# A hybrid decoder block on one core: w_out streamed twice beside the retrieval, once for the second token tile and once for the last two

## The chip, the cores and the metric

The kernel is one program on one core of a Trainium2 chip, everything in fp32. The time is the device time of one execution in microseconds (us). The engines are TensorE (PE, with its weight loads PEld), VectorE (DVE), ScalarE (ACT), GpSimd (POOL) and the sync engine SP, which issues transfers; all transfers run on the core's 16 DMA engines.

## What is computed

There are 512 tokens of width 2048 (four tiles of 128 tokens). The part of the reference that matters here, after attention and the convolution branch:

```
merged = sigmoid(gates)[attn] * attn + sigmoid(gates)[conv] * conv     # gates: h @ w_in (4096 columns)
y = merged @ w_out                                                     # 2048 x 2048
x = x + gate1 * rms_norm(y, g[1])
h = rms_norm(x, g[2]) * (1 + scale2) + shift2
q = h @ w_q                                                            # 2048 x 2048
s1, s2 = q halves . sub_keys; top-16 of each, top-16 of the 256 sums   # per token and head: 16 experts, 8 heads
act = gelu(h . expert_down[idx]) * softmax(top)
out = x + gate2 * rms_norm(act @ expert_up[idx], g[3])
```

For each token 128 rows of 2048 numbers are gathered from expert_down and 128 from expert_up, both tables in HBM.

## The kernel before

**Retrieval.** The 512 tokens are 512 blocks: one block gathers 128 rows of 8 KB from the down table (a [128, 2048] tile) and 128 from the up table. Positions within a block hold pairs of tokens and experts so that 32 blocks (a group J) finish 32 tokens. GpSimd issues the gathers in one order (down of block i, then up of block i - 22, L595). VectorE does one dot per block (`dot`, L1636), ScalarE the GELU and the small diagonal weights (L1173), TensorE the weighted sum of up rows (`weighted_rows`, 24 positions behind the dot). At each 32nd position `h2_quarter` turns 32 tokens of h into rows in four steps that alternate between TensorE and ScalarE (L1161), and the next dot waits for them. The gathers go into rings of three slots each, and of five from block WIDE = 168 on, which also waits for the end of the tail.

**Tails.** What lies between attention and the queries runs per token range, weights streamed from HBM in chunks of 1 MB through a ring of three (`rows`, `put` on SP; `group` on PE). `tail(0)` handles tile 0 (128 tokens), before any retrieval. `tail(1)` handles tiles 1 to 3 (384 tokens) while tile 0's 128 blocks are retrieved: for four column groups cg the gates ga and gc (w_in), the branch projections ao and co; then four groups of the output projection "out" (w_out, 16 chunks); then the norm chain: root of the sum of squares, scaling of y (L1732), residual with the turned x rows ("x", L1739), squares of the new x (L1260), their sums (PE), scaling (L1748), modulation (L1265). Then the queries "q" and scores "sc" (w_q, 16 chunks) for tile 1, each group of which VectorE routes at once (`route`, six steps, and `gates`); and again "q2" and "sc2" for tiles 2 and 3, which are routed later, each beside the blocks of the tile before it: from block 36 of the tile on, one pair of heads per 23 blocks (ROUTE, STRIDE), a step every second block.

**Order.** All engines run in program order. `block_pace` makes a table PACE: after chunk i of tail(1) every engine advances the retrieval up to position PACE[i] (`chunk_out` on PE, `passed` on ACT and DVE), by a weight per chunk: 12 for ga, gc, co and out, 6 for ao, 9 for x, 4 for q. Blocks 0 to 128 are spread over all chunks up to the first four of q, 763 units; 12 more chunks of q take blocks 128 to 138, the 16 chunks of q2 blocks 138 to 162. SP only stores finished rows between chunks (`behind`).

## Time and profile before

| | |
|---|---|
| median of 3 runs (us) | 4072.42 (4071.71 to 4079.16) |
| profiled execution (us) | 4070.52 |
| its span (us) | 4068.7 |
| busy: PE, PEld, DVE, ACT, POOL (us) | 2782.0, 1644.1, 2275.8, 539.8, 1408.8 |
| moved by DMA | 1430.07 MB, mean 351 GB/s |
| mean granted TensorE clock | 0.772 of 2.4 GHz |

A time "into the span" counts from the first instruction. Block 0's dot starts at 1159.86 us, block 128's at 2018.74, the first of the last tile (384) at 3371.88, and the last one at about 4001. In views of stretches "(x)" is a count of instructions; a product in fp32 is two instructions on PE. The share of DMA can be slightly above 1.

### The profile page before, as it was taken

Reading aid. Unit: us, or ns where it says so; the run is one execution under the profiler, and the core shown is the slowest. Engines: PE = TensorE matmul, PEld = TensorE weight load, DVE = VectorE, ACT = ScalarE, POOL = GpSimd, SP = SyncE. Lnnn points to the kernel's source line nnn. Section 1 sums busy time; section 2 is a strip of 40 time slices with the busy share of each in tenths; the row PEclk is TensorE's granted clock in tenths of the full one; section 3 lists DMA queues with packets and bytes.
Section 4 is the critical chain, followed back from the end, with each engine's and each line's share of the span. In section 5 each row is a group of like instructions: output and inputs, shape, how many; then the busy total and the mean of one; then the engine's idle time right before and its main releaser. Section 6 shows DMA issues by size and latency. Waiting matters only on the chain.

```text
span 4068.7 us, 38721 instructions
## 1 busy us (share of the span) xinstructions
PE 2782.0 (68%) x15652; PEld 1644.1 (40%) x15652; DVE 2275.8 (56%) x3525; ACT 539.8 (13%) x1203; POOL 1408.8 (35%) x1109
## 2 busy tenths in 40 slices
PE   5899899889899999998779344443443444444435
PEld 3687788789855554554657010110110100101100
DVE  5399789743474443435673666654656664444442
ACT  3211221200210011111211010010010100100000
POOL 2421211010023444333133563444435434444342
PEclk8999999999999999999989555555555555555556
DMA  9353424698669999999799999999999999999998
GB/s 365 144 218 134 156 90 170 239 407 342 223 243 373 400 419 397 414 379 400 282 370 402 400 422 421 421 421 422 421 421 419 415 422 416 421 422 419 422 421 368
DMA packets 204145, 1430.07 MB, mean 351 GB/s; under 512 B 24640, under 2 KB 24768, under 8 KB 32192
## 3 DMA queue, kind: packets, MB, share of 16 engines
q0 software_dynamic: 152064, 1107.36, 65.8%
q1 hardware_dynamic: 45984, 308.30, 19.5%
q10 hardware_dynamic: 5920, 11.94, 0.8%
q8 instruction: 124, 2.03, 0.2%
q14 instruction: 53, 0.43, 0.0%
HBM read 1420.13 MB, written 7.39 MB: 351 GB/s over the span
## 4 chain that ended last, share of the span: by engine, by line
PE 41%; DMA 39%; DVE 12%; POOL 3%; issue 3%; ACT 2%; ACTq 0%; DVEq 0%; SPq 0%; POOLq 0%
PE psum L624 40%; DMA front<-in_down,back 27%; DMA front<-in_up,back 10%; DVE front L1636 3%; POOL front L595 3%; DVE back L1403 2%; DVE back L1372 1%; DMA front<-in_w_in 1%; DMA back<-in_ada_w 1%; ACT back L1161 1%; DMA back<-in_up,back 1%; DMA back<-in_x 1%; DMA front<-in_w_conv_o 0%; DVE back L1739 0%; ACT front L1265 0%
## 5 line engine op out<-in xcount | busy, mean ns | idle before, releaser
L624 PE MATMUL psum<-front 128*32 128x512 f32 (+3 forms) x7136 | 1384.9, 615 | 862.9 <-DMA front<-in_up,back 793.9
L1636 DVE CUSTOM_DVE_ANT_0 front<-front,back 128x2048 f32<-128x2048 f32 x512 | 1171.1, 2292 | 1308.8 <-DMA front<-in_down,back 1201.6
L624 PEld LDWEIGHTS psum<-front 128*32 128x32 f32 (+1 forms) x7136 | 627.0, 162 | 1558.3 <-issue 1336.3
L595 POOL DMA_INDIRECT front<-in_down,back x512 | 606.7, 1185 | 897.7 <-DVE back L1636 626.2
L595 POOL DMA_INDIRECT front<-in_up,back x444 | 531.7, 1197 | 900.8 <-PE psum L624 860.5
L624 PE MATMUL psum<-back,front 128*32 128x128 f32 (+3 forms) x4384 | 625.5, 445 | 296.9 <-DMA back<-in_up,back 169.0
L624 PEld LDWEIGHTS psum<-back,front 128*32 128x32 f32 (+1 forms) x4384 | 365.0, 163 | 565.9 <-issue 317.2
L573 POOL TENSOR_TENSOR w_low<-front,w_high 128x2048 fp32r<-128x2048 f32 x33 | 153.7, 4657 | 539.7 <-ACT w_high L1049 539.7
L624 PE MATMUL psum<-x_high,w_high 128*128 128x512 f32 x640 | 252.0, 394 | 8.4 <-POOL x_low L579 5.6
L624 PE MATMUL psum<-x_low,w_high 128*128 128x512 f32 x640 | 250.6, 392 | 0.0
L624 PE MATMUL psum<-x_high,w_low 128*128 128x512 f32 x640 | 250.5, 391 | 0.0
L624 PE MATMUL psum<-back 128*32 128x128 f32 (+5 forms) x1400 | 181.7, 390 | 57.6 <-ACT back L1260 14.8
L1173 ACT ACTIVATE front<-back 128x32 f32<-128x32 f32 x512 | 116.1, 308 | 725.8 <-DVE back L1645 725.8
L624 PEld LDWEIGHTS psum<-back 128*128 128x128 f32 (+1 forms) x1400 | 134.9, 184 | 135.6 <-issue 56.6
L1372 DVE SCALAR_TENSOR_TENSOR back<-back 128x512 f32<-128x512 f32 x232 | 160.3, 766 | 0.0
L1049 ACT ACTIVATE w_high<-front 128x2048 fp32r<-128x2048 f32 x52 | 99.6, 1916 | 454.7 <-PE psum L624 405.5
L1403 DVE SCALAR_TENSOR_TENSOR back<-back 128x512 f32<-128x512 f32 x120 | 145.1, 1209 | 7.0 <-DMA back<-in_ada_w 1.5
L624 PEld LDWEIGHTS psum<-x_high,w_high 128*128 128x128 f32 x640 | 121.3, 189 | 34.8 <-POOL x_low L579 6.2
L624 PEld LDWEIGHTS psum<-x_high,w_low 128*128 128x128 f32 x640 | 121.1, 189 | 25.6
L624 PEld LDWEIGHTS psum<-x_low,w_high 128*128 128x128 f32 x640 | 121.2, 189 | 24.8
L1161 ACT ACTIVATE back<-psum 128x512 f32<-128x512 f32 x64 | 38.2, 597 | 515.0 <-DVE back L1636 359.7
L595 POOL DMA_INDIRECT back<-in_up,back x68 | 74.1, 1090 | 91.9 <-PE psum L624 87.3
(160 smaller groups left out, 1672.5 us busy)
## 6 DMA issues: line engine op xcount, KB each, us to landing
front<-in_w_in SPq DMA_DIRECT2D x116, 1024.0 KB, 8.4
back<-in_ada_w SPq DMA_DIRECT2D x64, 1024.0 KB, 7.8
front<-in_w_q SPq DMA_DIRECT2D x48, 1024.0 KB, 6.9
front<-in_ada_rows POOLq DMA_DIRECT2D x32, 1024.0 KB, 13.1
front<-in_w_out SPq DMA_DIRECT2D x32, 1024.0 KB, 8.0
front<-in_w_conv_o SPq DMA_DIRECT2D x16, 1024.0 KB, 9.4
front<-in_w_attn_o SPq DMA_DIRECT2D x16, 512.0 KB, 8.8
front<-in_down,back POOLq DMA_INDIRECT x512, 20.8
```

What stands on the lines that cost most here:

```text
L573: nc.gpsimd.tensor_tensor(wl[s], ring[s], wh[s % 2].bitcast(fp32), ALU.subtract).then_inc(w_low_done, 1)
L595: nc.gpsimd.indirect_dma_start(out=row_, out_offset=None, in_=table[:, :], in_offset=bass.IndirectOffsetOnAxis(ap=idx4[:, t % 2, c:c + 1], ...
L624: return nc.tensor.matmul(o, a, b, start=start, stop=stop)
L1049: A(wh[s % 2], ring[s], ACT.Copy).then_inc(w_high_done, 1)
L1161: A(h2r[:, i * NT:(i + 1) * NT], ps[:, 7, :], ACT.Copy).then_inc(h2r_ready, 1)
L1173: A(diag[:, b % 32, :], same[:, 0:32], ACT.Copy, scale=actv[:, n % 2, b % 16:b % 16 + 1]).then_inc(diag_ready, 1)
L1372: last[c] = st.did(V.scalar_tensor_tensor(total, src, tap, total, ALU.mult, ALU.add))
L1403: ins = V.scalar_tensor_tensor(total, part, weight, total, ALU.mult, ALU.add)
L1636: V.tensor_tensor_reduce(d_row[s], d_row[s], h2r, 1.0, 0.0, ALU.mult, ALU.add, pre[:, b // 16 % 2, b % 16:b % 16 + 1]).then_inc(dots_done, 1)
```

## The change

The out groups, the x rows and the norm chain move into the loop over query ranges (QUERIES): for tile 1 alone first, then for tiles 2 and 3 together as "out2", x, q2, sc2. w_out is streamed once for each range, so three times in the kernel instead of twice. tail(1) has 115 chunks instead of 99. The pace changes with it: 617 units carry blocks 0 to 128, an out chunk of tile 1 has weight 4; the chunks of q for tile 1 carry the same blocks as before; out2's 16 chunks blocks 138 to 162, the two x chunks up to 164 and 167, q2's 16 chunks up to 191. The rings widen at block 200, routing of tiles 2 and 3 starts at block 64 of the tile before, one pair of heads per 15 blocks. The cut diff (ScalarE's and VectorE's parts are moved into the same loop in the same way, with `goes` counting ranges for the semaphore values):

```diff
-    out += [("out", i, 4) for i in range(4)] + [("x", t, 1) for t in range(TAIL[c][1] // P)]
-    for go, _, _ in QUERIES[c]:
+    for go, q0, qn in QUERIES[c]:
+        out += [("out" + go, i, 4) for i in range(4)]
+        out += [("x", t, 1) for t in range(q0 // P, (q0 + qn) // P)]
         out += [(kind + go, i, k) for i in range(4) for kind, k in (("q", 4), ("sc", 0))]
...
-WIDE = 168
+WIDE = 200
-ROUTE, STRIDE = 36, 23
+ROUTE, STRIDE = 64, 15
...
-    work = [k * (12 if kind in ("ga", "gc", "co", "out") else 6 if kind == "ao" else 9 if kind == "x" else 4) / max(k, 1)
-            for kind, _, k in tail_groups(1) for _ in range(k)][:-28]
+    work = [k * (12 if kind in ("ga", "gc", "co") else 6 if kind == "ao" else 9 if kind == "x" else 4) / max(k, 1)
+            for kind, _, k in tail_groups(1) for _ in range(k)][:-46]
     out = [round(128 * at / sum(work)) for at in itertools.accumulate(work)]
     out += 4 * [128] + [129, 130, 131, 132, 133, 135, 136, 138]
-    return out + [138 + 3 * (i + 1) // 2 for i in range(16)]
+    out += [138 + 3 * (i + 1) // 2 for i in range(16)] + [164, 167]
+    return out + [167 + 3 * (i + 1) // 2 for i in range(16)]
...
# SP
-                for i in range(4):
-                    for s in range(4):
-                        rows(w_out, i, s)
+                for _, q0, qn in QUERIES[c]:
+                    for i in range(4):
+                        for s in range(4):
+                            rows(w_out, i, s)
+                            behind(c)
+                    for t in range(q0 // P, (q0 + qn) // P):
+                        put(x_row, x[t * P:(t + 1) * P, :])
                         behind(c)
...
# PE
-                    if i == 0:
-                        pe.wait_ge(mix_ready, 16 * (c + 1))
-                        group(4, 4, mixT, mix_at, dve_took, VTOOK[c, "co", 3], before)
-                    else:
-                        group(4, 4, mixT, mix_at, act_took, ATOOK[c, "out", i - 1], before)
+                        if i:
+                            group(4, 4, mixT, mix_at, act_took, ATOOK[c, "out" + go, i - 1], before, tq)
+                        elif go:
+                            group(4, 4, mixT, mix_at, act_took, ATOOK[c, "sc", 3], before, tq)
+                        else:
+                            pe.wait_ge(mix_ready, 16 * (c + 1))
+                            group(4, 4, mixT, mix_at, dve_took, VTOOK[c, "co", 3], before, tq)
...
# DVE, retrieve
-                        if step == 20:
+                        if step == 14:
                             gates(t, n)
...
# DVE, tail: only the first range of a tail is routed in it
+                    for i in range(4):
                         passed(c, 4)
+                        if not go:
+                            dve.wait_ge(act_took, ATOOK[c, "sc", i] + 4)
+                            for step in range(6):
+                                route(c, i, step)
```

## Rows read from the trace of the kernel before

**Rows 1.** The page: GB/s moved in each of 40 equal slices.
```profile
GB/s 365 144 218 134 156 90 170 239 407 342 223 243 373 400 419 397 414 379 400 282 370 402 400 422 421 421 421 422 421 421 419 415 422 416 421 422 419 422 421 368
```

**Rows 2.** Stretches: length, busy us of each engine (instructions), clock, DMA share, GB/s.
```profile
1150.00:1170.00 20.00, 20.00 (x64) 11.79 (x63) 15.99 (x45) 1.17 (x1) 5.59 (x3) 1.00 0.35 122
1170.00:1260.00 90.00, 90.00 (x281) 52.95 (x280) 54.57 (x71) 8.00 (x21) 28.64 (x20) 1.00 0.88 337
...
1320.00:1340.00 20.00, 17.85 (x190) 10.06 (x192) 7.54 (x7) 5.17 (x7) 6.50 (x4) 1.00 0.79 315
1340.00:1500.00 160.00, 159.28 (x652) 82.19 (x645) 65.19 (x69) 17.90 (x51) 67.89 (x54) 1.00 1.01 419
1500.00:1550.00 50.00, 47.85 (x298) 25.73 (x298) 21.69 (x26) 3.89 (x6) 14.84 (x12) 1.00 0.92 375
...
1700.00:1800.00 100.00, 97.32 (x515) 52.24 (x514) 33.86 (x32) 14.25 (x38) 37.01 (x28) 1.00 0.95 375
...
1940.00:1970.00 30.00, 15.23 (x93) 11.40 (x92) 13.74 (x9) 12.80 (x23) 1.88 (x2) 0.77 0.15 57
1970.00:2100.00 130.00, 108.08 (x849) 85.85 (x846) 103.58 (x385) 18.89 (x60) 35.14 (x27) 0.89 0.94 377
...
2120.00:2230.00 110.00, 104.13 (x576) 78.71 (x575) 40.70 (x38) 14.11 (x49) 40.82 (x34) 1.00 1.01 422
2230.00:2260.00 30.00, 14.00 (x189) 5.85 (x187) 9.23 (x9) 5.68 (x15) 12.55 (x11) 0.76 0.70 283
2260.00:4000.00 1740.00, 718.66 (x4430) 161.89 (x4430) 970.35 (x1485) 158.68 (x486) 784.33 (x694) 0.54 1.01 420
...
1150.00:1900.00 750.00, 735.60 (x3156) 392.52 (x3154) 314.17 (x357) 81.82 (x210) 291.89 (x220) 1.00 0.95 387
```

**Rows 3.** Timeline: start, us, engine, line; a block, a 384-column chunk, a 256-column chunk's loads.
```profile
1503.45 1.07 PE L624 MATMUL psum<-front 128*32 128x512 f32 x8
1504.45 10.59 PE L624 MATMUL psum<-back,front 128*128 128x384 f32 x32
...
2222.41 6.77 PEld L624 LDWEIGHTS psum<-front 128*128 128x128 f32 x32 [0.84 <-issue]
```

**Rows 4.** Groups by shape, 1958 to 1978: four chunks of 128 columns.
```profile
L624 PE MATMUL psum<-front 128*128 128x128 f32 x128 | 16.7, 295 | 14.8 <-ACT front L1265 14.8
```

**Rows 5.** Transfers issued, 1150 to 1900.
```profile
front<-in_w_out SPq DMA_DIRECT2D x16, 1024.0 KB, 8.5
```

**Rows 6.** Timeline of the norm chain of 384 tokens.
```profile
1905.19 6.76 DVE L1732 TENSOR_TENSOR front<-front,back 128x1536 f32<-128x1536 f32 x4
1911.99 4.22 DVE L1739 SCALAR_TENSOR_TENSOR back<-front,back,psum 128x128 f32<-128x128 f32 x16
...
1932.05 12.06 PE L624 MATMUL psum<-back 128*128 128x384 f32 x32 [7.78 <-ACT back L1260]
...
1949.14 9.68 ACT L1265 ACTIVATE front<-front,back 128x384 f32<-128x384 f32 x16 [4.41 <-DVE front L1748]
...
1965.65 0.94 POOL L595 DMA_INDIRECT front<-in_up,back  x1 [35.38 <-PE psum L624]
```

**Rows 7.** Timeline of VectorE: the dots of blocks 20, 127, 128, 160 and 192.
```profile
1252.79 2.28 DVE L1636 CUSTOM_DVE_ANT_0 front<-front,back 128x2048 f32<-128x2048 f32 x1
...
1977.64 2.29 DVE L1636 CUSTOM_DVE_ANT_0 front<-front,back 128x2048 f32<-128x2048 f32 x1 [19.11 <-DMA front<-in_down,back]
...
2018.74 2.29 DVE L1636 CUSTOM_DVE_ANT_0 front<-front,back 128x2048 f32<-128x2048 f32 x1
...
2238.47 2.29 DVE L1636 CUSTOM_DVE_ANT_0 front<-front,back 128x2048 f32<-128x2048 f32 x1 [10.28 <-ACT back L1161]
...
2405.88 2.29 DVE L1636 CUSTOM_DVE_ANT_0 front<-front,back 128x2048 f32<-128x2048 f32 x1 [6.29 <-ACT back L1161]
```

**Rows 8.** Stretches of 10 us, columns as in rows 2.
```profile
2110.00:2120.00 10.00, 5.45 (x18) 3.20 (x19) 4.60 (x4) 0.00 (x0) 8.55 (x5) 0.53 1.00 413
2170.00:2180.00 10.00, 8.00 (x44) 6.18 (x40) 3.67 (x4) 1.11 (x4) 4.66 (x4) 1.00 1.01 422
```

More of the change, by code:

```diff
@@ L941, in squares @@
                     for i in range(count):
-                        ins = mm(ps[:, 6, 0:n], ones, buf[:, i, 0:n], first and i == 0, last and i == count - 1)
+                        ins = mm(ps[:, 6, 0:buf.shape[2]], ones, buf[:, i, :], first and i == 0, last and i == count - 1)
                     return ins
@@ L968, in tail @@
                         modulation_columns(2)
-                for i in range(4):
-                    def before():
-                        if i:
-                            pe.wait_ge(act_took, ATOOK[c, "out", i])
-                            squares(sqt, 4, i == 1, False).then_inc(sqs_used, 1)
-                    if i == 0:
-                        pe.wait_ge(mix_ready, 16 * (c + 1))
-                        group(4, 4, mixT, mix_at, dve_took, VTOOK[c, "co", 3], before)
-                    else:
-                        group(4, 4, mixT, mix_at, act_took, ATOOK[c, "out", i - 1], before)
-                    if c == 0 and i == 0:
-                        modulation_columns(3)
@@ L982, in tail @@
-                pe.wait_ge(act_took, ATOOK[c, "out", 3] + 4)
-                squares(sqt, 4, False, True).then_inc(ss_done, 1)
-                for t in range(t0 // P, (t0 + n) // P):
-                    r = x_row[chunk_in()]
-                    for m in range(4):
-                        if t > t0 // P:
-                            pe.wait_ge(dve_took, VTOOK[c, "x", t - t0 // P - 1] + m + 1)
-                        for k in range(4):
-                            ins = nc.tensor.transpose(ps[:, m, k * P:(k + 1) * P], r[:, (4 * m + k) * P:(4 * m + k + 1) * P], ident)
-                        ins.then_inc(g_done, 1)
-                    chunk_out(c)
@@ L1204, in retrieve @@
                         z_std(J)
[L1205 removed]
+                    t, at = b // 128 + 1, b % 128 - ROUTE - 10
                     if 2 <= t < TT and at >= 0 and at % STRIDE == 0 and at < 4 * STRIDE:
@@ L1241, in tail @@
                     passed(c, 5)
-                for i in range(4):
-                    passed(c, 3)
-                    for m in range(4):
-                        act.wait_ge(g_done, DONE[c, "out", i] + m + 1)
-                        A(hT[:, 4 * i + m, tok], ps[:, m, 0:n], ACT.Copy)
-                        if i == 0 and m == 0:
-                            act.wait_ge(mix_ready, 16 * (c + 1))
-                        if i and m == 0:
-                            act.wait_ge(sqs_used, 10 * c + i)
-                        A(sqt[:, m, 0:n], ps[:, m, 0:n], ACT.Square).then_inc(act_took, 1)
-                    passed(c, 1)
@@ L1744, in tail @@
-                dve.wait_ge(std2_ready, 2 * c + 2)
-                dve.wait_ge(dve_took, VTOOK[c, "x", n // P - 1] + 4)
-                st.link(V.reciprocal(row[:, 0:n], row[:, 0:n]))
-                for i in range(4):
-                    V.tensor_tensor(hT[:, 4 * i:4 * i + 4, tok], mixT[:, 4 * i:4 * i + 4, tok],
-                                    row[:, 0:n].unsqueeze(1).to_broadcast(wide), ALU.mult).then_inc(h2n_ready, 1)
-                for i in range(4):
-                    passed(c, 4)
-                    dve.wait_ge(act_took, ATOOK[c, "sc", i] + 4)
-                    for step in range(6):
-                        route(c, i, step)
-                    if i:
-                        gates(c, i - 1)
```

137 lines of the change are left out of this document (86 added, 51 removed).

## The prediction

> **What bounds the kernel now.** I read the page's slices first [rows 1]: from slice 24 of 40 on the rate stays at about 421 GB/s. From 2260 us to 4000 us the transfers are the bound: 420 GB/s over 1740 us [rows 2]. A block there costs 2.10 MB (128 rows of 8 KB from each table), which is 4.97 us at 422 GB/s. What can move is therefore how many bytes the kernel carries, and how long the queues stand below 422 GB/s before 2260 us.
>
> The stage table [rows 2] gives that second sum. The lost time of a stretch is its length times (1 - rate/422). 1150 to 1170: 14.2 us; 1170 to 1260: 18.1; 1320 to 1340: 5.1; 1500 to 1550: 5.6; 1700 to 1800: 11.1; the rest up to 1900 about 8, so that the one row of 1150 to 1900 (387 GB/s) gives 62. Then 1940 to 1970: 26.0 (57 GB/s); 1970 to 2100: 13.9; 2120 to 2230: nothing; 2230 to 2260: 9.9. That is some 112 us up to 2260. Outside that total nothing is to be had from moving work.
>
> TensorE looks as bound as the queues in the second tail: 735.6 us busy of 750 [rows 2]. Its piece costs [rows 3]: a chunk of 16 products of 384 tokens 10.59 us as one piece (10.24 us from start to start at 0.32 us per instruction), a block 1.07 us. A chunk with its 2.01 blocks is then 12.4 us of TensorE, and 1.05 + 2.01 x 2.10 = 5.27 MB or 12.5 us of DMA. The two limits coincide: taking TensorE work out of this stretch lets it run no faster than 422 GB/s.
>
> **The change, part by part.**
>
> *The extra load.* w_out is streamed twice beside the retrieval instead of once: 16 more chunks of 1024 KB (the stretch before shows 16 of them, the page 32 in all) [rows 5], 16.8 MB, at 422 GB/s **+39.8 us**. All of it goes into a stretch that ran at 422 GB/s (2120 to 2230) or into new stretches of the same kind, so no idle bandwidth hides it. The x rows are loaded as often as before, only later; the third load of w_q was there already (48 chunks). Bounds 35 to 40: the lower one if a chunk or two fall into the gaps that remain.
>
> *Gates, branches and the first tile's output projection (up to the first norm chain).* By the pacing formula the 128 blocks are now spread over 617 units instead of 763, so a 12-unit chunk has 2.49 blocks, not 2.01. Per chunk DMA is 1.05 + 2.49 x 2.10 = 6.27 MB, 14.9 us; TensorE 10.24 + 2.66 = 12.9 us. The out chunks have 128 columns (16.7 us for four, so 4.2 us each [rows 4]) and 0.83 block: 5.1 us of TensorE against 6.6 us of DMA. TensorE gets slack of about 2 us a chunk, but the bytes up to the chain are the same. What is recovered is only lost DMA time. In 1170 to 1260 VectorE halts after block 19 until the first branch sum is ready; block 20 starts at 1252.79 [rows 7], behind ten chunks of TensorE work, and the rate falls there. It will have up to five more dots to do before that wait, 5 more gathers of 1.05 MB, 12 us at most; I take 9. The stalls at each 32nd block (1320, 1500, 1700 stretches, 21.8 us together) come from four copies in series, some 7 us, behind a full chunk; with bursts of 2.5 blocks more is in flight when they begin, with rings of the same three slots. I take 8 of the 21.8. The 14.2 us before the first gathers stay. Sum **-17 us**; bounds 0 (three-slot rings refill no better, or bursts of three blocks drain them) and -45 (everything but the 14.2 and 3 of the rest goes).
>
> *The first chain (norm of y, residual, norm of x2, modulation), now for 128 tokens.* Before [rows 6]: scaling 6.76 from 1905.19 on, three residual groups of 4.22 with dots between, eight squares with their sums 12.06, then reciprocal and second scaling, modulation 9.68 us up to 1958.8: with the root and the reciprocal ahead of the scaling some 60 us. GpSimd waited 35.38 us for TensorE before its next up gather, because the gathers are issued in order; queued work lasted about 10 us of it, and 26.0 us were lost. With a third of the tokens: 0.9 + 2.4 + one group 4.2 + sums about 6 + 0.9 + 0.6 + modulation 4.5, plus semaphores about 3: 23 us, and a gap between up gathers of about 20 us. Less the 10 us (up to 17 with the rings freshly requested) 3 to 10 us stay lost: **-20 us**; bounds -15 and -26.
>
> *Routing of the second tile* (from block 127 at 1977.64 to block 138, about 2100) has the same instructions in the same order in both. Two routes and a gates step fill VectorE from there to block 128 at 2018.74 [rows 7]. Its loss, 13.9 us, stays: **0** (+-3).
>
> *The second projection, for 256 tokens, beside blocks 138 to 162.* Per chunk TensorE has 6.8 us (weight loads of one chunk in the last query group [rows 3]) plus 1.5 blocks, 8.4 us; DMA 1.05 + 1.5 x 2.10 = 4.2 MB, 9.95 us. Exactly this mix ran at 422 GB/s and clock 1.00 [rows 2]. TensorE's, ScalarE's and VectorE's work of this part costs nothing while that holds; the cover gone, it would be 16 x (8.4 - 5.1), 53 us of TensorE, less what the first part gave up.
>
> *The second chain, for 256 tokens, between blocks 162 and 168.* It is new as a stall. 1 + 1.7 + 4.5 + 4.2, then two dots, 4.2, three dots (2.29 each, but 5 us each by DMA); squares 8 x 1.03; 0.8 + 1.7 + 1.1; modulation 16 x 0.42 = 6.7 us; then one chunk of 6.8 us before the next block. Between up gathers lies a gap of 21 to 29 us. With the same 10 to 17 us of queued transfers: **+12 us**; bounds +4 (dots and gathers interleave so well that all is covered) and +26 (what the chain lost before).
>
> *Block 192's stall.* The turning of rows at each 32nd block meets three-slot rings at 160 and 192 now, since the rings grow to five slots at block 200, not 168. At 160, where the weights ended, it cost 9.9 us (the dot idle 10.28 us behind ScalarE [rows 7]). Now the end of the weights falls on 192 and costs that, and 160 has weights in flight: **+4 us**; bounds 0 and +9.
>
> *Routing of tiles three and four, 15 blocks a head pair instead of 23.* Steps stay two blocks apart within a pair. Two routes and a gates step took 39 us [rows 7], so about 18 us each, 21 with gates: 4 x 21 + 60 dots x 2.29 = 221 us in 60 blocks x 4.97 = 298 us. Rings of five slots and DMA hide it: **0**; bounds 0 and +4.
>
> Sum: 39.8 - 17 - 20 + 12 + 4 = **+19 us**. The profiled execution took 4070.5 us (span 4068.7), the median of the runs is 4072.4, 1.9 above it. So 4089.5 in the profile, **4091 us** as a median.
>
> A page differs from a row here. The rate of mixed weights and gathers is 422 GB/s [rows 2]. The Trainium skill, "DMA: Bandwidth & Descriptors", Where 436 GB/s comes from, says that transfers between HBM and SBUF are held by the HBM side at about 358 GB/s per core. By that the reload would be an estimated 46.9 us and the sum +26; the trace's 422 decides.
>
> **Rivals.** (a) *The first stretch was starved by TensorE* and the queues fill once it has slack. For it: 735.6 of 750 us busy, and losses scattered in it. Then -45 there, -26 for the first chain and +4 for the second: 39.8 - 45 - 26 + 4 + 4 = -23 us, 4049 us. It decides as soon as the first part recovers over 36 us at my other terms. Against: the stretch 1340 to 1500, 160 us long, loses 1 us as it is. (b) *The second chain costs what the first did.* Nothing of it is covered, because GpSimd's in-order gathers stop with TensorE: 39.8 - 10 - 15 + 26 + 9 = +50 us, 4122 us. For it: the 35.38 us wait. Against: 256 tokens and blocks inside it. (c) *TensorE's clock falls in the new 128-column out chunks*, where it now waits for weights. With TensorE busy 5.45 of 10 us the granted clock was 0.53 of 2.4 GHz, near the 1.2 GHz level; with 8.00 of 10 us it was 1.00 [rows 8]. The share would be 5.1 of 6.6, between them, nearer the second. At 1.2 GHz a chunk has 8.4 + 0.83 x 2.14 = 10.2 us against 6.6: 16 x 3.6 = +57 us, 4148 us at worst, half of it if the clock comes and goes. The Trainium skill, "TensorE: Matmul & The Clock Gate", HAM oscillation, says that when the products of a slice are shorter than the wait for the next slice, each slice starts at the low clock; by that rule this rival holds. Against it stands the second projection's mix at clock 1.00, whose TensorE share is 8.4 of 9.95. (d) *The change doesn't do what it says:* the gates stretch follows TensorE's removed work (16 x 6.1 = 98 us shorter). The coincidence of both limits excludes nearly all of this.
>
> **Numbers.** About 0.2% (8 us) can be told from no change. My forecast's own terms, 4075 to 4105: 0.60; (a), or a part of it that ends below 4064: 0.15; between them, near no change: 0.10; (b): 0.10; (c) 0.04; (d) 0.01. The range, 4056 to 4120, takes in the nearer half of (a) and of (b). Of the forecast's share about 0.1 lies within 0.2%: faster 0.16, same 0.20, slower 0.64.
>
> **What would show it.** The free run from block 200 on must keep 4.97 us a block and 420 GB/s. The bytes rise by 16.8 MB, from 1430 to 1447. The stretch before the first chain ends 5 to 20 us sooner (last square at 1880 to 1895 instead of about 1898) with DMA at 395 GB/s or more. The wait of GpSimd in the first chain falls from 35 to about 20 us. A second gap of GpSimd of 20 to 30 us appears between blocks 162 and 168, near 2230 us. Block 192 comes at about 2425 us, against 2405.88 [rows 7], and the difference stays the same to the end. I am wrong if the first stretch shortens by more than 35 us, if the second chain shows no dip, if the clock falls below 0.8 in the out stage, or if the later blocks run slower than 5.02 us.

## The result and the profile after

The changed kernel took 4120.58 us (median of 4 runs, 4113.18 to 4121.15) beside 4074.18 of the kernel before: ratio 1.011 [1.0097, 1.0122], some 46 us slower. The forecast was +19 us and 4091; the direction was right, the size was not. The profiled execution, 4113.18 us with a span of 4111.4, was the shortest of the four, so the profiles differ by 42.7 us in span. A further set of runs of the same kernel gave 1.0089 [1.0075, 1.0102] (e5 below).

The page of the changed kernel: GB/s in 40 slices, the transfers as a whole, and one issue row.
```profile
GB/s 366 139 225 130 154 102 146 270 404 330 206 273 396 416 376 414 374 421 361 381 392 395 353 381 419 419 421 422 421 421 420 418 421 417 419 421 420 421 422 368
DMA packets 206455, 1446.94 MB, mean 352 GB/s; under 512 B 24896, under 2 KB 25024, under 8 KB 32448
...
front<-in_w_out SPq DMA_DIRECT2D x48, 1024.0 KB, 8.7
```
w_out is issued 48 times and the bytes rose by 16.87 MB, as forecast. Beside [rows 1] the slices agree within 3 GB/s from slice 25 on, so the difference lies before about 2500 us.

Stretches of the changed kernel, with the columns of [rows 2].
```profile
1150.00:1170.00 20.00, 20.00 (x63) 11.78 (x62) 18.94 (x57) 1.95 (x3) 4.10 (x2) 1.00 0.19 63
1170.00:1260.00 90.00, 80.86 (x247) 46.42 (x246) 55.81 (x68) 8.93 (x26) 38.04 (x27) 0.94 0.98 387
...
1500.00:1550.00 50.00, 45.52 (x260) 24.61 (x261) 16.48 (x16) 5.71 (x9) 20.05 (x16) 0.93 0.87 349
1690.00:1800.00 110.00, 91.02 (x465) 48.87 (x462) 42.31 (x45) 10.64 (x27) 41.79 (x34) 0.91 0.93 379
1150.00:1900.00 750.00, 658.12 (x3169) 369.56 (x3168) 319.04 (x372) 79.57 (x216) 280.78 (x223) 0.94 0.96 390
1900.00:1940.00 40.00, 17.75 (x124) 14.26 (x122) 25.99 (x41) 11.85 (x34) 4.86 (x6) 0.66 0.70 292
1940.00:1970.00 30.00, 29.85 (x259) 26.78 (x258) 16.29 (x60) 2.80 (x11) 2.82 (x3) 1.00 0.90 343
1970.00:2100.00 130.00, 98.82 (x708) 73.16 (x707) 102.01 (x344) 19.87 (x60) 48.08 (x35) 0.84 0.94 377
2100.00:2210.00 110.00, 102.82 (x606) 75.77 (x608) 38.41 (x36) 14.81 (x46) 38.87 (x32) 0.98 1.01 421
2210.00:2240.00 30.00, 19.97 (x152) 10.02 (x143) 23.37 (x44) 3.17 (x5) 12.88 (x11) 0.73 0.87 352
2240.00:2260.00 20.00, 9.98 (x40) 6.18 (x40) 12.76 (x14) 9.04 (x15) 3.75 (x4) 0.76 1.00 415
2260.00:2280.00 20.00, 14.33 (x57) 11.16 (x58) 5.44 (x5) 7.32 (x20) 1.88 (x2) 0.73 0.18 64
2300.00:2420.00 120.00, 116.11 (x641) 86.20 (x643) 45.31 (x42) 20.59 (x75) 42.10 (x36) 0.97 1.01 421
2420.00:2480.00 60.00, 23.49 (x216) 7.74 (x208) 33.27 (x75) 9.66 (x27) 25.53 (x21) 0.59 0.88 353
2480.00:4040.00 1560.00, 641.23 (x3980) 144.99 (x3980) 875.30 (x1353) 142.29 (x427) 717.18 (x625) 0.54 1.01 420
```
The free run kept its 420 GB/s. Read as lost time (length times (1 - rate/422)): the stretch up to 1900 lost 57 us against 62; the first chain (1900 to 1970) 17.9 against 29 by the same reading of the kernel before; routing (1970 to 2100) 13.9 against 13.9; the second output projection nothing; the stall at block 160 (2210 to 2240) 5.0 against 9.9; the new second chain (2260 to 2280) 17.0; block 192 (2420 to 2480) 9.8, where the kernel before lost nothing (421 and 422 GB/s from 2380 to 2440). The table in the prediction leaves out two stretches of the kernel before: 1900 to 1940 (390 GB/s, 3.0 us) and 2100 to 2120 (306 GB/s, 5.5 us); with them its 112 us agree with the 120.3 below.

Two rows cover the whole stretch, the first of the kernel before, the second of the changed one.
```profile
1150.00:2560.00 1410.00, 1131.24 (x5736) 619.35 (x5738) 724.65 (x1267) 171.28 (x466) 560.39 (x430) 0.87 0.95 386
```
```profile
1150.00:2560.00 1410.00, 1142.19 (x6178) 699.67 (x6176) 682.94 (x1159) 186.08 (x521) 522.63 (x412) 0.88 0.94 385
```
Lost time 120.3 and 123.6 us. The balance closes: 16.87 MB at 422 GB/s, 40.0 us, and 3.3 us more of lost time make 43.3; block 256 came 44.0 us later, block 511 42.7. The forecast had 21 us less lost time, net, and it became 3 us more. Note what such a balance is: bookkeeping. Every run moved 420 GB/s from 2560 to 4000, so the bytes and the lost time before 2560 have to add up to the delay. It says where the time went; it doesn't say why.

The norm chains of the changed kernel in the timeline: first the one of 128 tokens, then the one of 256.
```profile
1909.43 2.29 DVE L1642 CUSTOM_DVE_ANT_0 front<-front,back 128x2048 f32<-128x2048 f32 x1 [7.02 <-DMA front<-in_down,back]
...
1912.63 2.50 DVE L1740 TENSOR_TENSOR front<-front,back 128x512 f32<-128x512 f32 x4
...
1915.16 4.22 DVE L1747 SCALAR_TENSOR_TENSOR back<-front,back,psum 128x128 f32<-128x128 f32 x16
...
1927.90 6.26 ACT L1274 ACTIVATE front<-front,back 128x128 f32<-128x128 f32 x16 [1.75 <-DVE front L1756]
...
1934.21 12.05 PE L626 MATMUL psum<-front 128*128 128x128 f32 x79 [8.46 <-ACT front L1274]
...
1942.02 0.94 POOL L597 DMA_INDIRECT front<-in_up,back  x1 [19.21 <-PE psum L626]
...
2221.29 4.63 DVE L1740 TENSOR_TENSOR front<-front,back 128x1024 f32<-128x1024 f32 x4
...
2245.84 8.12 PE L626 MATMUL psum<-back 128*128 128x256 f32 x32
...
2257.64 7.98 ACT L1274 ACTIVATE front<-front,back 128x256 f32<-128x256 f32 x16 [3.08 <-DVE front L1756]
...
2265.67 24.66 PE L626 MATMUL psum<-front 128*128 128x256 f32 x110 [11.71 <-ACT front L1274]
...
2276.73 0.94 POOL L597 DMA_INDIRECT front<-in_up,back  x1 [26.86 <-PE psum L626]
...
2285.71 2.29 DVE L1642 CUSTOM_DVE_ANT_0 front<-front,back 128x2048 f32<-128x2048 f32 x1 [20.27 <-DMA front<-in_down,back]
```
GpSimd's wait in the first chain fell from 35.38 [rows 6] to 19.21 us, as forecast, and a second one of 26.86 appeared. The dots [rows 7] have as counterparts in the changed kernel:
```profile
1953.20 2.29 DVE L1642 CUSTOM_DVE_ANT_0 front<-front,back 128x2048 f32<-128x2048 f32 x1 [19.11 <-DMA front<-in_down,back]
...
1994.31 2.29 DVE L1642 CUSTOM_DVE_ANT_0 front<-front,back 128x2048 f32<-128x2048 f32 x1
...
2214.89 2.29 DVE L1642 CUSTOM_DVE_ANT_0 front<-front,back 128x2048 f32<-128x2048 f32 x1 [8.68 <-ACT back L1165]
...
2440.40 2.29 DVE L1642 CUSTOM_DVE_ANT_0 front<-front,back 128x2048 f32<-128x2048 f32 x1 [8.68 <-ACT back L1165]
```
Blocks 127 and 128 came 24.4 us sooner, 160 23.6 sooner, 192 34.5 later, and 200 42.0 later (2440.8 and 2482.7).

Two cautions on reading such positions. First, a block is a measure of progress only where both kernels have moved the same other bytes ahead of it. At block 128 nearly all is equal (16 w_out chunks issued since 1150 in both), but of x the kernel before has loaded three rows of 1 MB and the changed one only one: the other two now come behind block 162. These 2.1 MB are 5.0 us that moved and weren't won. So about 19 us of lost time were won up to there, which agrees with the rates (869 us at 375 GB/s lost 96.8, 844 us at 383 GB/s 78.0). Second, single profiles scatter. Nine profiles whose code is the changed kernel's up to block 128 have it 19.2 to 27.7 us sooner than the profile of the kernel before (mean 23.3), and five of the kernel before, with the same code up to there, have it 0 to 9.3 us later (mean 6.1). By the means the lead is 29 us and not 24.

### The profile page after: what moved, and what is told of

It reads as the page before. It is cut to its first block, busy times and chain, and to the rows that moved or that the text cites. A ratio compares the mean times of both kernels' runs of the same rounds, so it can differ in the third digit from the quotient of the medians.

```text
span 4111.4 us, 39974 instructions
## 1 busy us (share of the span) xinstructions
PE 2807.4 (68%) x16228; PEld 1732.3 (42%) x16228; DVE 2277.0 (55%) x3535; ACT 558.8 (14%) x1268; POOL 1406.7 (34%) x1109
## 4 chain that ended last, share of the span: by engine, by line
DMA 42%; PE 35%; DVE 12%; POOL 5%; issue 3%; ACT 2%; ACTq 0%; DVEq 0%; POOLq 0%
PE psum L626 35%; DMA front<-in_down,back 29%; DMA front<-in_up,back 10%; POOL front L597 4%; DVE front L1642 3%; DMA back<-in_up,back 2%; DVE back L1378 1%; DVE back L1409 1%; DMA front<-in_w_in 1%; ACT back L1165 1%; POOL x_low L581 1%; DVE back L1620 1%; DMA back<-in_x 1%; ACT front L1274 0%; DVE back L1578 0%
## 5 line engine op out<-in xcount | busy, mean ns | idle before, releaser
L626 PEld LDWEIGHTS psum<-front 128*128 128x128 f32 (+1 forms) x7184 | 632.0, 161 | 1549.0 <-issue 1302.2
L626 PE MATMUL psum<-back,front 128*32 128x128 f32 (+4 forms) x4848 | 645.3, 424 | 311.7 <-DMA back<-in_up,back 154.0
L626 PEld LDWEIGHTS psum<-back,front 128*32 128x32 f32 (+1 forms) x4848 | 439.4, 173 | 543.5 <-issue 334.5
L626 PE MATMUL psum<-back 128*32 128x128 f32 (+5 forms) x1464 | 184.0, 381 | 53.5 <-ACT back L1269 12.3
```

Of the source, the lines that this page charges most:

```text
L626: return nc.tensor.matmul(o, a, b, start=start, stop=stop)
```

## Experiments

Ratios are to the kernel before, run on the same chip. "Balance" is (bytes over those of the kernel before)/422 plus the change of lost time between 1150 and 2560 (each good to about 2 us, since rates have whole GB/s), beside how much later block 256 was in the profile. The runs that are not in the table have their times in the text.

| run | median us | ratio [95%] | lost us | balance | block 256 |
|---|---|---|---|---|---|
| before | 4074.18 | 1 | 120.3 | 0 | 0 |
| changed | 4120.58 | 1.011 [1.0097, 1.0122] | 123.6 | +43 | +44.0 |
| e5 again | 4116.21 | 1.0089 [1.0075, 1.0102] | 123.6 | +43 | +44.3 |
| e1 small reload | 4108.16 | 1.0077 [1.0059, 1.0095] | 153.7 | +36 | +37.6 |
| e9 light products | 4122.01 | 1.0101 [1.0084, 1.0118] | 133.6 | +53 | +53.5 |
| e10 both | 4103.41 | 1.0057 [1.004, 1.0073] | 150.4 | +33 | +35.4 |
| e3 retrieval in chains | 4108.38 | 1.0077 [1.0059, 1.0095] | 120.3 | +40 | +40.3 |
| e11 split chain | 4120.00 | 1.0098 [1.0081, 1.0114] | 170.4 | +50 | +48.3 |
| e12 split, covered | 4086.64 | 1.0019 [1.0009, 1.0029] | 137.0 | +17 | +16.6 |
| e13 widened at 193 | 4123.27 | 1.0113 [1.0098, 1.0129] | 133.6 | +53 | +53.5 |
| e14 covered, paced | 4114.64 | 1.0091 [1.0077, 1.0105] | 123.6 | +43 | +44.9 |
| e16 covered, 1.25 | 4121.35 | 1.0104 [1.0088, 1.0121] | 123.6 | +43 | +43.4 |
| e17 covered, 1.75 | 4099.57 | 1.0065 [1.0051, 1.0079] | 106.9 | +27 | +27.7 |
| e18 uncovered, 1.75 | 4119.49 | 1.0102 [1.0087, 1.0116] | 133.6 | +53 | +54.4 |

The balance closes in every row within 3 us, as it must while the free run keeps its rate. What remains to be found is what sets the lost time.

**The changed kernel again: e5,** on another chip, without an edit.


> The changed kernel once more, to have its time on the chip of the other three of this group. Theory: 4118 to 4122; if it comes out near 4110, part of what the first group of experiments seemed to win (12 us each) was only the chip.

Its span was 4110.6 us and its blocks stood where they stood in the first profile (block 192 34.4 us late, block 256 44.3), so the shift is the kernel's. The ratio puts it at 36 to 46 us.

**Is it the bytes or the work? e1, e9, e10.** e1 loads only a corner of each w_out chunk of out2; e9 has a quarter of its products; e10 does both.
```diff
-                            rows(w_out, i, s)
+                            if go:
+                                put([r[:, 0:1, 0:P] for r in tring], w_out[i, s][:, 0:1, 0:P])
+                            else:
+                                rows(w_out, i, s)
...
-  group(4, 4, mixT, mix_at, act_took, ATOOK[c, "sc", 3], before, tq)
+  group(4, 1, mixT, mix_at, act_took, ATOOK[c, "sc", 3], before, tq)
```


> The changed kernel, but the 16 chunks of w_out for the last two tiles are loaded as 64 KB instead of 1024 KB each (128 columns of one k; the products run as before on what else lies in the buffers, so the last two tiles' projection is wrong). 15.7 MB less. Theory A (the added bytes are paid in full, because the queues are the bound wherever no chain stops them): 37 us less than the changed kernel's 4120, so 4083, with about the same lost DMA time. Rival B (the added time is late routing, late widening of the rings and TensorE's rearranged work, the bytes fall into gaps): 4105 or more.

> The changed kernel with only one of the four products per chunk and output column block in the second projection (16 chunks of w_out for the last two tiles: 64 instead of 256 products, all bytes loaded; the projection of those tiles is then incomplete). Theory F (the second projection meets two limits at once, TensorE at 8.9 us and the queues at 9.95 us a chunk with its 1.5 blocks, so that taking one away wins next to nothing): 0 to 6 us less than the changed kernel. Rival G (TensorE alone is the bound there): 20 us or more less.

> The same with, in addition, the 16 chunks loaded as 64 KB each. Theory F: now both limits are gone, 24 blocks take some 120 us instead of 155, so 30 to 38 us less than the changed kernel, some 4080; the sum of the two single experiments (about 10 us) is far exceeded. Rival G: about as much as taking the products alone.

e1 took away 15.7 MB, 37 us of transfers, and won 5 to 13 us (1.0077 against the 1.0089 and 1.011 of the changed kernel). Its stretches:
```profile
2100.00:2140.00 40.00, 40.00 (x208) 29.39 (x207) 16.19 (x15) 3.59 (x12) 21.49 (x14) 1.00 0.96 364
2140.00:2200.00 60.00, 59.11 (x354) 44.40 (x356) 22.21 (x21) 9.97 (x32) 22.14 (x19) 1.00 0.95 368
```
Without the bytes TensorE is busy for 99.11 of 100 us and DMA drops to 364 and 368 GB/s. e9, without the work, kept 422 GB/s with TensorE busy 57.66 of 110 us and won nothing, as expected. In e10 both limits were lifted, and still only 13 to 21 us came, not the 30 to 38 expected: blocks 144 to 156 ran at about 5.1 us each, but the second chain behind them stalled as before (255 GB/s from 2240 to 2290). So the second output projection stands on both limits at once, and half of the price or more (23 of 36 to 46 us) is left without it.

**The two small edits: e2, e6, e7** (each to the kernel before).
```diff
-WIDE = 168                 # e2, e6
+WIDE = 200
-ROUTE, STRIDE = 36, 23     # e2, e7, with the steps that follow from it
+ROUTE, STRIDE = 64, 15
```


> The kernel before with only the constants of the change: rings widen at block 200 instead of 168, routing of tiles 3 and 4 from block 64 at one head pair per 15 blocks, its gates at step 14. Theory A: routing is hidden, the three-slot rings cost up to 9 us at block 192; 4074 to 4083. Rival B (late routing and late widening carry a good part of the 46 us): 4090 or more.

> The kernel before with the rings widened at block 200 instead of 168, nothing else. Theory C (the 9 us of the constants come from the turning of rows at block 192 meeting rings of three slots): 4081 to 4084. Rival D (they come from denser routing steps): 4074 to 4076.

> The kernel before with routing of tiles 3 and 4 from block 64 on at one head pair per 15 blocks, rings widened at 168 as before. Theory C: 4073 to 4077, since five slots and the queues hide routing. Rival D: 4081 to 4084.

e2 gave 4085.2 us, 1.0022 [1.0012, 1.0032]; e6 4090.31, 1.002 [1.0011, 1.0029]; e7 4081.43, 1.0001 [0.9992, 1.001]. Late routing is free, as forecast; late widening costs the kernel before 8 us. In e6's profile it appears at one place: the difference is 9.6 us at block 192, all of which was there at block 160 already, before the edit acts, and 15.7 at block 196. The up ring widens by its own block number, 22 places later in GpSimd's order than the down ring: WIDE = 168 put it at place 190, just ahead of the turning of rows at 192, WIDE = 200 puts both rings behind it. Which of the two rings matters wasn't separated.

**The first chain: e4 and e3.** Both retrieve blocks inside the chain, where the code otherwise lets TensorE and ScalarE wait; e4 is the kernel before with it, e3 the changed one, in both chains.
```diff
+                    if c == 1:
+                        retrieve(170 if go else 128)
```


> The kernel before with the same continuation up to position 128 in its one chain of 384 tokens. Theory A: of the 26 us lost at 1940 to 1970 about 14 are won, 4060. Rival B: no difference, 4072 to 4076.

> The changed kernel with the retrieval going on inside both norm chains of the second tail: after the eight sums of squares TensorE, and after the second root ScalarE, go on to position 128 (first chain) or 170 (second) before they wait for the modulated h. Theory A (the queues run empty in the chains because the next up gather waits for TensorE, which stands in its program order at the query product): GpSimd's waits of 19.2 and 26.9 us shrink to 5 to 12 us, 15 to 25 us are won, 4098. Rival B (VectorE's residual, dots and scaling hold the gathers as long as TensorE does): under 5 us won, 4116 or more.

e4: 4072.82 us, 0.9995 [0.9985, 1.0004], nothing. Block 127 came 14.3 us sooner (1963.3), block 128 1.8 us later: the likely reason is that from block 127 on the path is VectorE's routing, which begins when the chain's queries are there, so that gathers covered in the chain are waited for anyway. In e3 block 170 came 19.6 us sooner than in the changed kernel (15.3 ahead of the kernel before instead of 4.3 behind), and at block 192 only 4 us of that were left; of the 15 to 25 us expected at the end, 5 to 13 came by the ratios.

**A chain split without a second load: e8, e11, e12.** w_out is loaded once, for 384 tokens; only the norm chain and the queries are split in two ranges. e8 retrieves inside both chains and keeps 14 blocks back for them; e11 is the plain form; e12 adds retrieval inside both chains, a pace that follows it, and an up ring that widens at GpSimd's place 176.
```diff
-WIDE = 173
+WIDE, UWIDE = 176, 154
-    out += [123, 124, 126, 127, 128] + 4 * [128] + [129, 130, 131, 132, 133, 135, 136, 138]
-    return out + [140, 143] + [143 + 3 * (i + 1) // 2 for i in range(16)]
+    out += [123, 127, 127, 128, 128] + 4 * [128] + [129, 130, 131, 132, 133, 135, 136, 138]
+    return out + [141, 144] + [148 + 3 * (i + 1) // 2 for i in range(16)]
+MID = {"": (124, 126), "2": (146, 148)}      # retrieve(MID[go][..]) behind squares 4 and 8
```


> w_out streamed once for all 384 tokens as in the kernel before, but the norm chain and queries in two ranges as in the change (tile 1, later tiles 3 and 4 beside blocks 138 to 172), with the retrieval going on inside the chains and 114 instead of 121 blocks ahead of the first; rings widen at 180, routing from block 48, one head pair per 19 blocks. Theory A (the shorter first chain stands on the path to the second tile's routing and its 25 us are real; what the change loses is the second projection with its reload, 40 to 50 us of queue and TensorE time in one): block 128 some 30 us sooner than in the kernel before, 10 to 18 us kept at the end, 4056 to 4066. Rival E (the second chain and the pieces around it give back all that the first wins, whatever the reload): 4072 or more.

> The change without its second projection: w_out streamed once, for 384 tokens, paced as before; the norm chain and queries in two ranges as in the change (x and chain of tiles 3 and 4 between blocks 138 and 143, their queries up to 167), rings widened at 173, routing from block 44, one head pair per 20 blocks. Theory A: block 128 about 25 us sooner than in the kernel before, the second chain costs 15 to 18, late widening 5: within 5 us of the kernel before, and some 40 us under the changed kernel. Rival E (the split chain itself is what costs): 4090 or more.

> The same with the retrieval going on inside both chains (to 124 and 126, to 146 and 148, the pace of the last 16 chunks moved up by as much) and the ring of the up rows widened at its block 154, that is at position 176 together with the other one instead of 22 positions later. Theory A: the second chain's stall mostly gone and nothing lost at block 192: 10 to 18 us under the kernel before, 4058 to 4066. Rival: as e11.

e8: 4106.63 us, 1.0064 [1.0052, 1.0077], nothing of the hoped gain: blocks kept back did not speed a stretch in which TensorE was busy 723.41 of 750 us (1170 to 1920), and block 128 came 5.6 us later than in the kernel before, where 30 us sooner was expected. e11: 4120.00 us where a time near the kernel before was expected. It carries the bytes of the kernel before and costs what the change costs: its second chain stands behind routing in VectorE's order, DMA moved 259 GB/s from 2060 to 2140, and from block 138 to block 148 it fell back by 22.7 us (from +7.0 to +29.7 against the kernel before). e12 (the diff is against e11; its routing starts at 48, one pair per 19 blocks) took 33 us off that, with the same bytes and the same arithmetic: 11 us of it stood at block 138, behind the first chain, 41 at block 148. It is still 8 us slower than the kernel before, where 10 to 18 us faster was expected. So most of what e11 costs depends on how the stalls are covered, though cover, pace and ring widening changed together here.

**The second chain of the changed kernel itself: e13 to e18.** e13 only widens the rings as the tail ends; e15 widens the kernel before's up ring where its down ring widens.
```diff
-WIDE = 200
+WIDE, UWIDE = 193, 171      # e13; e15: 168, 146
```


> The changed kernel with the five-slot rings as soon as its second tail ends: the down ring at block 193 instead of 200, the up ring at the same place of GpSimd's order (index 171 instead of 200, which was place 222). In the changed kernel alone a comparison of the old tile with both settings gave +6 us at blocks 192 to 196. Theory W (the late widening costs 8 us in the changed kernel too): block 200 comes 5 to 9 us sooner than in the changed kernel and the gain stays; ratio to before 1.007 to 1.0085, that is 4109 to 4115 us beside a before of 4081. Theory V (the stall of block 192 falls on three-slot rings in either case, since the second tail ends at block 191, so that only what follows can gain): 0 to 3 us, ratio 1.009 to 1.011.

> The kernel before with the up ring widened where the down ring is (GpSimd's place 168, not 190). If the three-slot up ring behind block 168 costs anything in it, block 192's stall of 9.6 us shrinks by 2 to 6 us: ratio 0.9985 to 0.9995. If the widening only has to come ahead of the turn at block 192 (place 190 does), nothing: ratio 0.9995 to 1.0005.

e13 won nothing and its block 192 was worse (2420 to 2460 lost 13.7 us by its rows of 330 and 225 GB/s, the changed kernel 9.8). Its trace shows a likely reason: GpSimd stood idle for 14.83 us ahead of the gather at 2450.82, until VectorE's dot of block 192 (2448.26 to 2450.55). With WIDE = 193 the widened down ring begins with slot 0, which block 192 had taken just before, so block 193's rows couldn't be requested until that dot was done, and the other table's gathers stood behind it. With 200 slot 0 was last taken by block 198, one block further back. e15: 4077.94 us, 1.0003 [0.9994, 1.0012], no effect; the ring only has to be wide ahead of the turn. So this way of widening early doesn't win back the stall at 192; a setting without the clash of slots wasn't run.

e14, e16 and e17 put retrieval to blocks 169 and 171 inside the second chain (e14 in the first too). They differ in the pace of the 16 query chunks behind it: 1.5, 1.25 and 1.75 blocks each. The down ring widens at 196, 200 and 204, the up ring at the same place of GpSimd's order. e18 is 1.75 without the retrieval, widened at 200.
```diff
-    return out + [167 + 3 * (i + 1) // 2 for i in range(16)]
+    return out + [171 + 5 * (i + 1) // 4 for i in range(16)]   # e16; e14: 3 // 2; e17: 7 // 4; e18: 167 + 7 // 4
+MID = (169, 171)
+                        if go and kk % 4 == 3:
+                            retrieve(MID[kk // 4])
```


> The changed kernel with both w_out loads, but with retrieval steps inside its second chain (to block 169 behind the fourth square, to 171 behind the last), the pace of the last query chunks moved behind them (the second tail ends at block 195, not 191), and the up ring widened at GpSimd's place 196. In the split kernel with one load of w_out the same edits took away 33 us. Theory S (the new second chain with its drained three-slot rings is, beside the bytes, what the change costs): the same edits take 20 to 30 us here too; ratio 1.003 to 1.005, 4093 to 4101 us beside a before of 4081. Theory T (the second output projection with its bytes and products is what costs, and the queues are given no room to catch up): 0 to 10 us, ratio 1.008 to 1.010, as when only the retrieval was continued.

> The changed kernel with its first chain as it is and retrieval inside the second chain only (to block 169 behind the fourth square, to 171 behind the last); the 16 last query chunks have 1.25 blocks each behind block 171, so that the second tail ends at block 191 as in the changed kernel; down ring widened at 200 as there, up ring at the same place of GpSimd's order instead of 222. In e14 the window 2210 to 2300 lost 8 us of transfers against 23 in the changed kernel, but the first chain, where retrieval was also put, lost 9.5 more (block 128 at -14.9 against -24.4) and the 192 turn 5 more. Theory S (the second chain's stall is worth some 15 us once the queues have something behind it): block 200 at +24 to +30 against before, ratio 1.0055 to 1.0075, 4099 to 4107 us beside a before of 4076. Theory T (the chain's loss is a catch-up that TensorE, busy all the time afterwards, gives back): block 200 at +38 to +42, ratio 1.009 to 1.011.

> As e16, but 1.75 blocks instead of 1.25 for each of the 16 last query chunks behind block 171 (the second tail ends at block 199); routing of the later tiles from 72 on, 14 blocks a head pair; rings widened at 204. In e16 the chain was covered (block 172 at -19.4 against before, the changed kernel +10.6), and then TensorE was busy for 100.00 of 100 us from 2280 to 2380 at 313 to 421 GB/s and all was given back by block 192. Theory U (both limits coincide behind the chain, so the covered stall is worth something only if DMA and not TensorE is the limit afterwards): with 1.75 blocks a chunk DMA wants 11.2 us a chunk and TensorE about 9.9; the queues keep 420 GB/s to block 192, and block 208 comes at +22 to +32 against before, ratio 1.005 to 1.0075. Theory T (the stall is always given back, by another stall at the end of the tail): block 208 at +38 or more, ratio 1.009 or more.

> The changed kernel with its chain uncovered and only the pace of the last 16 query chunks at 1.75 blocks (end of the tail at block 195, routing from 68, 14 blocks a head pair, rings widened at 200). Behind the chain the changed kernel already ran at 422 GB/s for 120 us, so both theories expect next to nothing: block 208 at +36 to +44, ratio 1.009 to 1.0115. If it were much faster (under 1.007), TensorE would have been the limit behind the uncovered chain too.

The cover worked each time: block 170 came at -9.0, -18.6 and -19.7 us against the kernel before (e14, e16, e17), where the changed kernel has +4.3. What became of it was decided behind the chain. Stretches of e16, then of e17:
```profile
2260.00:2280.00 20.00, 8.25 (x37) 5.45 (x30) 15.32 (x13) 10.27 (x27) 7.71 (x4) 0.66 0.94 391
2280.00:2300.00 20.00, 20.00 (x102) 14.68 (x101) 4.60 (x4) 0.00 (x0) 5.65 (x4) 1.00 0.81 313
2300.00:2340.00 40.00, 40.00 (x208) 31.18 (x208) 10.50 (x9) 4.51 (x16) 15.15 (x12) 1.00 0.91 361
2340.00:2380.00 40.00, 40.00 (x222) 30.58 (x224) 12.59 (x13) 8.62 (x29) 12.74 (x10) 1.00 1.01 421
2380.00:2420.00 40.00, 38.53 (x266) 29.14 (x258) 17.61 (x17) 7.68 (x28) 17.28 (x13) 1.00 0.93 371
```
```profile
2260.00:2280.00 20.00, 8.47 (x32) 6.37 (x33) 15.47 (x14) 9.67 (x24) 7.48 (x4) 0.66 0.87 361
2280.00:2300.00 20.00, 20.00 (x106) 14.14 (x104) 3.75 (x4) 0.00 (x0) 6.68 (x6) 1.00 0.84 318
2300.00:2340.00 40.00, 35.33 (x191) 26.43 (x189) 13.80 (x12) 4.82 (x14) 16.87 (x13) 1.00 1.01 422
2340.00:2380.00 40.00, 34.34 (x210) 24.07 (x210) 13.89 (x13) 8.41 (x30) 14.22 (x14) 0.96 1.01 422
2380.00:2420.00 40.00, 33.08 (x239) 24.27 (x237) 15.31 (x15) 4.99 (x17) 10.66 (x10) 0.88 1.01 420
```
In e16 TensorE is full from 2280 to 2380 and DMA falls to 313 and 361 GB/s: the queues were ahead and had to wait for it, and by block 192 the 23 us had shrunk to 3.8, of which 3.3 had been there at block 128 already. In e17 each chunk carries more blocks, TensorE has air, the queues stay at 420 to 422 from 2300 to 2420, and part of the lead stays to the end: 4099.57 against 4119.49 us for e18 on the same chip, 20 us by the medians and 15 by the ratios. The only difference between these two is the cover, with a tail, ring widening and routing that come 4 blocks later for it. e18 shows that the pace alone is worth nothing. e14, between the two in pace, lost what it won at two places of its own: block 128 came 9.6 us later than in the changed kernel, probably because retrieval stands ahead of the first chain's last sums, and 2420 to 2460 lost 14.7 us. Its tail ended behind block 192, and its widening at 196 has e13's clash of slots (GpSimd idle 7.42 us at 2457.45 behind block 195's dot).

No version beat the kernel before. The nearest relatives of it, e4, e7 and e15, are equal to it; the best of the changed kernel, e17, is 0.65% slower.

## Why the prediction was right in its direction and wrong in its size

- **The extra load, +39.8: right as an amount of transfer** (16.87 MB, 40.0 us). Its price isn't the bytes alone: e1 won 5 to 13 of 37 us when they were taken away, because the projection's products fill TensorE to the same length. The forecast said that the two limits coincide, but drew from it only that nothing is won by relief of TensorE in the first part; it holds for the added part as well, and from both sides (e1, e9).
- **The first part, -17: the first failed term.** 5 us came out of it net (62 to 57, by the rates of 387 and 390 over 750 us in [rows 2] and after); the means of five profiles of the kernel before and nine of the changed one up to block 128 give 8.5 (384.4 and 389.2 GB/s). The start did nearly what was forecast: 1170 to 1260 lost 18.1 and now 7.5 us, less 3 us more from 1150 to 1170 (122 and 63 GB/s). But of the stalls at each 32nd block, of which I took 8 us as won, nothing came: the first lost 5.1 and now 3.3 us (1300 to 1330 at 376 GB/s), 1500 to 1550 lost 5.6 and now 8.6, 1690 to 1800 now 11.2 with 1700 to 1800 having lost 11.1 [rows 2]. TensorE did get its slack, 658.12 busy of 750 us against 735.60. Block 112 came 18.1 us sooner and block 120 only 6.8, but that is no gain lost again: at its block 112 the changed kernel had issued 8 chunks of w_out and the kernel before 15, and those 7 chunks are 17.4 us. No run tested these turns alone; that slack on TensorE does not shorten them is what the trace shows, why is open.
- **The first chain, -20: the mechanism right, the size half.** The 35.38 us wait became 19.21, as forecast; the loss fell from 29 to 17.9 us. What failed is the cover: I had the queued transfers last 10 to 17 us, and they lasted 5. GpSimd's wait began at 1922.8, and the rate was 236 GB/s from 1925 to 1930 and 0 behind it. VectorE had come to the chain late, held by dots that waited for DMA (7.02 us at 1909.43), and the modulation of 128 tokens took 6.26 us, not 4.5; why so little was queued is open. Rows of 5 us from the times at which the queues ran dry: in the kernel before (wait begun at 1930.3), then in the changed kernel's first and second chain (begun at 1922.8 and 2249.9):
```profile
1935.00:1940.00 5.00, 5.00 (x16) 2.88 (x16) 0.00 (x0) 3.37 (x4) 0.00 (x0) 0.99 0.79 328
1940.00:1945.00 5.00, 4.11 (x13) 2.14 (x12) 0.24 (x1) 2.27 (x3) 0.00 (x0) 1.00 0.01 3
```
```profile
1925.00:1930.00 5.00, 0.75 (x7) 0.55 (x5) 4.17 (x8) 2.47 (x7) 0.00 (x0) 0.96 0.56 236
1930.00:1935.00 5.00, 0.79 (x3) 0.79 (x4) 4.09 (x4) 5.00 (x15) 0.00 (x0) 0.50 0.00 0
...
2255.00:2260.00 5.00, 0.00 (x0) 0.00 (x0) 4.96 (x5) 2.35 (x5) 0.00 (x0) 0.73 0.94 390
2260.00:2265.00 5.00, 0.00 (x0) 0.00 (x0) 5.00 (x4) 5.00 (x11) 0.00 (x0) 0.50 0.03 11
```
  The test that I set, last square at 1880 to 1895, failed too: it was about 1900. The test was also wrong in itself: by the new pace 123 blocks stand ahead of the last chunk of out instead of 121, 10 us more of transfers, which "the bytes up to the chain are the same" overlooks.
- **Routing of the second tile, 0: right.** 1970 to 2100 lost 13.9 us in both, block 128 shifted with block 127 (-24.4 both), and block 138 came 25.9 us sooner.
- **The second projection, 0 while covered: right for DMA,** 421 GB/s from 2100 to 2210 at clock 0.98. I had put TensorE at 8.4 of 9.95 us a chunk. It was busy 102.82 of 110 us, 9.3 a chunk. From 2120 to 2200 its groups by shape show why:
```profile
L626 PE MATMUL psum<-back,front 128*128 128x256 f32 x272 | 61.0, 382 | 0.0
L626 PE MATMUL psum<-front 128*32 128x512 f32 x96 | 12.8, 603 | 3.4 <-ACT front L1177 2.4 <-issue 0.8
L626 PE MATMUL psum<-back 128*128 128x256 f32 x16 | 3.8, 379 | 0.0
```
The 32 instructions of a chunk took 7.2 us and not 6.8 (61.0 for 272), a block 1.07 (12.8 for 12) as forecast, and the sums of squares, which I had left out, 0.45 a chunk. The forecast took its 6.8 us from the weight loads of one chunk; the kernel before already had 66.7 us for 297 such instructions (2130 to 2220), 0.224 us each as here.
- **The second chain, +12 (+4 to +26): within its bounds, but too low by 6 us.** 2240 to 2300 lost 18.4 us (415, 64 and 399 GB/s). The wait of 26.86 us is near the upper end of the forecast's 21 to 29, and the queued work covered 10 us of it (423 and 390 GB/s up to 2260, then 11), the lower end of 10 to 17. e17 against e18 measures the part that more cover gives back: 15 us in the ratios (1.0102 - 1.0065 is 0.0037 of 4077).
- **Block 192 and the late widening, +4 (0 to +9): right.** 9.8 us of loss there, less the 4.9 us that block 160's stall gave back (9.9 before, 2210 to 2240 now 5.0), is +4.9. But 7.5 us of delay came between blocks 192 and 200 (+34.5 to +42.0), where the forecast said that the difference would stay the same. e6 measured the widening alone, without that gain at block 160, at 8 us.
- **Late routing, 0: right** (e7).

Summed up at blocks: ahead of block 128, 37 us of lost time were to be won (17 + 20), and about 19 were, since of the lead of 24.4 us 5.0 are the two x rows that moved behind it. From block 128 to the end I had +56 (39.8 + 12 + 4), and +62 was measured (-24.4 to +42.7, less the same 5.0). So 18 us of the miss lie in the first two terms and 6 in the second chain. By the means of the profiles the first shortfall is about 13 us instead of 18. The forecast of lost time was -21 us, and the balance says +3: a miss of 24 us in the profile. The rest of the miss of 29 us is that the profiled execution of the changed kernel was 7 us under its median, which no term of the forecast could know.

**The rivals.** (b), a second chain that costs like the first, gave 4122 us, and its terms are the nearest to what the traces show (first part -10, chains -15 and +26, block 192 +9; measured about -5, -11, +18, +5). But its condition isn't met: 10 of the 26.86 us were covered, so its time, nearer to the measured one than the forecast's, is in part luck. I held 256 tokens and the blocks inside the chain against it; the wait was indeed 26.86 us and not 35.38. (a) failed: relieved TensorE did not fill the queues. (c) did not come: 1800 to 1900, the 128-column chunks, ran at a clock of 0.91 with TensorE busy 82.54 us, and 2100 to 2210 at 0.98, both nearer 2.4 than 1.2 GHz. The Trainium skill, "TensorE: Matmul & The Clock Gate", HAM oscillation, speaks of slices whose products are shorter than the wait for the next slice. By the forecast's own numbers a chunk had 5.1 us of products and blocks and 1.5 us of waiting, so the prediction was wrong to say that (c) holds by that rule. No run here had such slices; this case neither bears the rule out nor contradicts it.

## What to carry to other kernels

When two engines stand at their limits at once, keep a balance: bytes over the free rate plus the time in which the queues ran below it; an edit is worth only what it changes in that sum, and a lead won in one stretch was given back in the next one where TensorE had no air (e16) and kept in part where it had (e17). Before you count on queued transfers to cover a serial chain, look at how long they last from the moment at which the issuing engine stops; with three slots per ring they lasted 5, 9 and 10 us of waits of 19, 35 and 27 us here. Before you read a lead from the position of a block, count what else had been moved by then: 7 chunks in another order look like 17 us of gain. A prefetch depth that changes at some block must come ahead of the next known stall, for each queue in its own order, and must not begin with the slot that was filled last (e13).

## What was unexpected

- A 23 us lead can vanish without any new wait that stands out: in e16 it went in a hundred microseconds in which TensorE was simply never idle.
- A product's time didn't scale with its columns: 61.0 us for 272 instructions of 256 columns are 0.224 us each, where two thirds of the 0.32 us of 384 columns would be 0.213.
- e11, with no additional byte, was as slow as the change: 170.4 us of lost time instead of 120.3, the largest single part (22.7 us between blocks 138 and 148) at a chain that stood behind routing on VectorE.
